# Two products on one moving operand: high and low activations side by side in the expert and FFN gate/up products

## The chip, the cores and the metric

One core of a Trainium2 chip runs the whole program in one launch. The metric is the device time of that launch in microseconds (us). The engines that matter are TensorE (PE, whose weight loads are listed as PEld), VectorE (DVE), ScalarE (ACT), GpSimd (POOL) and the DMA queue issued from SyncE (SP).

## The reference, cut to what matters

A sequence of 256 tokens with 1024 features passes through two blocks (latent attention with a PEER layer, gated linear attention with a PEER layer) and then a third block (two windowed attentions and a gated FFN). Everything is float32. The parts that the change touches:

```
def peer_ffn(x, w_query, sub_keys, u_tab, v_tab):     # twice; 128*128 experts, 8 heads, top 16
    ...                                               # query products, top-k, gates
    u = u_tab[idx]
    h = gelu(einsum('bthkd,btd->bthk', u, xi))
    w = gate * h
    return einsum('bthk,bthkd->btd', w, v_tab[idx])

u = silu(einsum('btd,df->btf', h, w_gate)) * einsum('btd,df->btf', h, w_up)   # FFN, 2816 hidden
x = x + einsum('btf,fd->btd', u, w_down)
```

## The kernel before, in words

**Weights as a stream of slabs.** All weights come through one stream of slabs of 128 x 1024 numbers (512 KB). SP loads slab n into one of 4 raw buffers. ACT makes its high part `hi` (`split_hi`, L248) in one of 3 buffers, once the slab three back is used up (semaphore `eaten`). DVE, or POOL for the PEER U slabs, makes the low part `lo` = raw - hi (`split_lo`, L257). Both parts are of the reduced-width float type fp32r. The activations are split in the same way into `xh` and `xl`, each of 8 chunks of 128 features x 256 tokens, by `Norm.high` (L349) and `Norm.low` (L356).

**PEER layer.** Instead of gathering experts it computes all of them: 8 query slabs, 128 U slabs and 128 V slabs per layer. `first(i)` on PE forms the 128 x 256 product of U slab i: for each of 8 chunks one matmul of `hi` with `xh` (L1245) and one of `hi` with `xl` (L1246), each with 256 moving columns; then, after a wait for `lo`, 8 matmuls of `lo` with `xh` (L1249). All 24 add up in the left half of PSUM bank i % 3, and the last one counts `eaten` up. During slabs 0 to about 40 DVE ranks the scores (`rank`).

**Gates, from slab 44 (LEAD).** Gates are built in 64 groups of 4 tokens. `GROUP_AT` gives a group to four of five slabs from 44 to 122, so a "group slab" has these steps: PE does 8 fp16 matmuls for the group (`sums`, L1272) after `first(i)`; DVE makes the one-hot tiles of the group two ahead (`one_hots`, L1502, L1504, L1506), multiplies the finished part of slab i by its gates (`gate_slab`, L1514) and applies the group's gates to all earlier slabs (`apply`, L1522). ACT does `split_hi` of the slab three ahead, then `bend(i)`: the Gelu of the product, of which the first `cut` tokens go back into PSUM in place (L1365) and the rest to `hidden` in SBUF (L1367). Then come `keep_sums` (L1373) and `low_gates` (L1384). `first(i)` may overwrite its bank when `gate_slab(i-3)` is done. `sums(g)` needs `one_hots(g)` and `low_gates(g)`, made two groups before.

**V slabs.** `second(v)` has 12 matmuls of 512 moving columns (L1285, L1286, L1292), with `pe_mh` and `pe_ml`, the split of `hidden[:, v]`, as weights.

**FFN.** The order of slabs is gate t, up t, down t-1, for 22 t. Gate and up are 24 matmuls of 256 columns each (`first` L2712, L2713 and `rest` L2720) into the two halves of bank t % 2; down is 12 of 512 columns (L2734 to L2736). ACT makes Silu of gate (L2770), DVE the product (L2787), ACT and DVE its split (L2774, L2790). All `split_lo` of the FFN are on DVE.

Other 512-column products are those of gated linear attention (`along`, L1702, L1704, L1710).

Of the kernel before, what the change touches and what calls it, by code (L numbers as in the profile page):

```python
# [17 lines left out]
P = 128  # L18
# [85 lines left out]
class Kernel:  # L104
    def __init__(self, nc, ctx, dram):
# [10 lines left out]
        self.xh = self.sb(ctx, "xh", [P, KD, T], F32R)  # L116
        self.xl = self.sb(ctx, "xl", [P, KD, T], F32R)
# [152 lines left out]
class Norm:  # L270
# [11 lines left out]
    def given_squares(self, act):  # L282
        k = self.k
        act.activation(k.xh[:, 0:4].rearrange("p c t -> p (c t)"), k.h[:, 0], ACT.Square, scale=D ** -0.5,
                       accum_out=k.mean[:, 0:1]).then_inc(self.squared.sem, 1)
# [8 lines left out]
    def given_diagonals(self, dve):  # L294
        k = self.k
        dve.tensor_tensor_reduce(
            out=k.xl[:, 0:4].rearrange("p c t -> p (c t)"), in0=k.h[:, 1], in1=k.h[:, 1], scale=1.0 / D, scalar=0.0,
            op0=ALU.mult, op1=ALU.add, accum_out=k.mean[:, 1:2]).then_inc(self.summed.sem, 1)
# [827 lines left out]
def peer(k, l, s0, norm, after):  # L1126
# [6 lines left out]
             "ranked", "turned", "equal", "hotted", "lowered", "summed", "spread", "applied", "bent", "gated", "m_hi", "m_lo")  # L1133
    (q_act, q_dve, zeroed, keyed, scored, s_act, s_dve, counted, raised, powered, ranked, turned, equal, hotted,
     lowered, summed, spread, applied, bent, gated, m_hi, m_lo) = (k.sig(f"pe_{x}") for x in names)
    hi, lo = k.hi, k.lo
    u0, v0, end = s0 + U0, s0 + V0, s0 + SLABS
    with ExitStack() as ctx:
# [8 lines left out]
        count = k.sb(ctx, "pe_count", [P, NK], I32)  # L1147

# [41 lines left out]
        with k.nc.Block() as block:  # L1190
# [11 lines left out]
            def _(pe):  # L1202
# [29 lines left out]
                def first(i):  # L1232
# [11 lines left out]
                    for c in range(KD):  # L1244
                        pe.matmul(ps, hi[:, r, c * P:(c + 1) * P], k.xh[:, c], start=(c == 0), stop=False)  # L1245
                        pe.matmul(ps, hi[:, r, c * P:(c + 1) * P], k.xl[:, c], start=False, stop=False)  # L1246
                    pe.wait_ge(*k.lo_at[u0 + i])
                    for c in range(KD):
                        last = pe.matmul(ps, lo[:, r, c * P:(c + 1) * P], k.xh[:, c], start=False, stop=(c == KD - 1))  # L1249
# [96 lines left out]
            def _(act):  # L1346
# [12 lines left out]
                def bend(i):  # L1359

                    g = grouped(i)
                    act.wait_ge(k.eaten, u0 + i + 1)
                    ps, cut = first_ps(i), g * GROUP
                    if cut:
                        last = act.activation(ps[:, 0:cut], ps[:, 0:cut], ACT.Gelu)  # L1365
                    if cut < T:
                        last = act.activation(hidden[:, i, cut:], ps[:, cut:], ACT.Gelu)  # L1367
# [66 lines left out]
            def _(dve):  # L1434
# [73 lines left out]

                def gate_slab(i):
# [36 lines left out]
                for i in range(LEAD, NK):  # L1546
                    g = GROUP_AT.get(i)
# [26 lines left out]
    gated.advance(NK - LEAD - 1)  # L1574
    for x in (equal, hotted, lowered, summed, spread, applied):
        x.advance(GROUPS)
# [516 lines left out]
def second_block(k, s0, norm, after):  # L2093
# [13 lines left out]
    with ExitStack() as ctx:  # L2107
# [73 lines left out]
        with k.nc.Block() as block:  # L2181
# [239 lines left out]
            def _(act):  # L2421
# [42 lines left out]
                for g in range(B2_SLABS):  # L2464
# [41 lines left out]
                    if g in (BB + 1, BB + 3):  # L2506
                        for m in ((g - BB - 1), (g - BB)):
                            act.wait_ge(y_done.sem, y_done.at(m + 1))
                            act.activation(k.xh[:, 2 * m:2 * m + 2].rearrange("p c t -> p (c t)"), yb[:, m], ACT.Copy)\
# [5 lines left out]
            def _(dve):  # L2515
# [60 lines left out]
                for g in range(B2_SLABS):  # L2576
# [44 lines left out]
                    if g in (BB + 1, BB + 3):  # L2621
# [8 lines left out]
                        for m in (2 * c, 2 * c + 1):  # L2630
                            dve.wait_ge(y_hi.sem, y_hi.at(m + 1))
                            dve.tensor_tensor(k.xl[:, 2 * m:2 * m + 2].rearrange("p c t -> p (c t)"), yb[:, m],
                                              k.xh[:, 2 * m:2 * m + 2].bitcast(F32).rearrange("p c t -> p (c t)"),
                                              ALU.subtract).then_inc(y_lo.sem, 1)
# [35 lines left out]
def ffn(k, s0, norm, out):  # L2670
# [3 lines left out]
    names = ("bent", "middle", "m_hi", "m_lo", "stepped", "done", "stored")  # L2674
    bent_up, middle, m_hi, m_lo, stepped, done, stored = (k.sig(f"ff_{x}") for x in names)
    order = ffn_order()
    end = s0 + len(order)
    with ExitStack() as ctx:
        bent = k.sb(ctx, "ff_bent", [P, 2, T])
        mid = k.sb(ctx, "ff_mid", [P, 2, T])  # L2680
        mh = k.sb(ctx, "ff_mh", [P, 2, T], F32R)
# [8 lines left out]
        with k.nc.Block() as block:  # L2690
# [14 lines left out]
            def _(pe):  # L2705
                def first(g, t, x, c0, c1):
# [3 lines left out]
                    for c in range(c0, c1):  # L2710
                        cols = slice(c * P, (c + 1) * P)
                        pe.matmul(first_ps(t, x), k.hi[:, r, cols], k.xh[:, c], start=(c == 0), stop=False)  # L2712
                        pe.matmul(first_ps(t, x), k.hi[:, r, cols], k.xl[:, c], start=False, stop=False)  # L2713

                def rest(g, t, x):
# [3 lines left out]
                    for c in range(KD):  # L2719
                        last = pe.matmul(first_ps(t, x), k.lo[:, r, c * P:(c + 1) * P], k.xh[:, c], start=False,  # L2720
                                         stop=(c == KD - 1))
                    last.then_inc(k.eaten, 1)
# [21 lines left out]
                for g, (kind, t) in enumerate(order):  # L2744
# [9 lines left out]
                    else:  # L2754
                        if kind == "gate" and t >= 2:
                            pe.wait_ge(middle.sem, middle.at(t - 1))
# [4 lines left out]
            def _(act):  # L2761
                norm.high(act, 0, KD)
                split_hi(k, act, s0 + 2)
                for g, (kind, t) in enumerate(order):
                    split_hi(k, act, s0 + g + RING)
                    if kind == "up":
                        act.wait_ge(k.eaten, s0 + g + 1)
# [9 lines left out]
            def _(dve):  # L2777
# [3 lines left out]
                for g, (kind, t) in enumerate(order):  # L2781
                    split_lo(k, dve, s0 + g + RING)
                    if kind == "up":
                        dve.wait_ge(bent_up.sem, bent_up.at(t + 1))
# [100 lines left out]
```

## Time and profile before

| | |
|---|---|
| median of 3 runs | 2291.86 us (2291.79 to 2295.11) |
| the profiled execution: its own time, its span | 2291.86 us, 2290.1 us |
| PE busy | 98% of the span |
| DVE, ACT, POOL busy | 61%, 54%, 31% |
| mean granted TensorE clock | 0.992 of full speed |

The profile's "busy" of PE counts each matmul from start to modelled end, and consecutive matmuls overlap, so 98% says only that PE is hardly ever without one. What a matmul costs in a dense stretch is the distance from its start to the next one's start.

### The profile page before, as it was taken

What the parts mean: (1) busy time and instruction counts of PE and PEld (TensorE: products, weight loads), DVE (VectorE), ACT (ScalarE), POOL (GpSimd) and SP (SyncE); (2) the same over time, 40 slices, a digit from 0 to 9 for tenths busy, and PEclk for the clock granted to TensorE, in tenths of its full rate; (3) what the DMA queues carried; (4) which work ended last, traced back from release to release, by engine and by line L of the source; (5) the groups of instructions that cost most, each with busy time, mean ns of one, the idle gap of its engine ahead of it and who ended that gap; (6) DMA issues with size and microseconds to landing.
All of it is one profiled execution on the core that took longest, in us unless ns stands there. A gap on an engine that the chain in (4) does not pass through costs nothing. (4 is left out here: it accounts for less than half of the span.)

```text
span 2290.1 us, 38835 instructions
## 1 busy us (share of the span) xinstructions
PE 2243.1 (98%) x15059; PEld 2025.1 (88%) x15059; DVE 1399.9 (61%) x2682; ACT 1236.2 (54%) x2448; POOL 704.2 (31%) x346
## 2 busy tenths in 40 slices
PE   8799999999999999999999999999999999999999
PEld 7679999999888888887999999988888888888998
DVE  6546965666555555565597566655555558446555
ACT  4434467777544444464446777754444454555443
POOL 3305877777200000001488777730000004000000
PEclk9889999999999999999999999999999999999999
DMA  5125655555566666563565555556666656424654
GB/s 166 56 66 162 183 177 161 162 162 159 180 185 186 190 186 187 153 179 109 156 183 178 160 164 159 165 175 185 187 189 185 188 162 225 124 85 162 187 185 148
DMA packets 122535, 375.55 MB, mean 164 GB/s; under 512 B 13024, under 2 KB 17376, under 8 KB 122352
## 3 DMA queue, kind: packets, MB, share of 16 engines
q1 hardware_dynamic: 122352, 373.06, 53.3%
q8 instruction: 121, 1.98, 0.3%
q14 instruction: 62, 0.51, 0.1%
HBM read 371.96 MB, written 1.05 MB: 163 GB/s over the span
## 5 line engine op out<-in xcount | busy, mean ns | idle before, releaser
L248 ACT ACTIVATE hi<-raw 128x1024 fp32r<-128x1024 f32 (+1 forms) x703 | 737.4, 1050 | 421.7 <-PE bank L1249 184.3
L257 DVE TENSOR_TENSOR lo<-raw,hi 128x1024 fp32r<-128x1024 f32 (+2 forms) x443 | 536.8, 1215 | 358.4 <-ACT hi L248 358.0
L257 POOL TENSOR_TENSOR lo<-raw,hi 128x1024 fp32r<-128x1024 f32 x260 | 630.7, 2429 | 252.8 <-ACT hi L248 252.8
L1245 PE MATMUL bank<-xh,hi 128*128 128x256 f32 x2048 | 512.3, 288 | 0.0
L1246 PE MATMUL bank<-xl,hi 128*128 128x256 f32 x2048 | 500.8, 283 | 0.0
L1285 PE MATMUL bank<-hi,pe_mh 128*128 128x512 f32 x1016 | 403.1, 397 | 1.1 <-DVE pe_ml L1528 1.1
L1286 PE MATMUL bank<-hi,pe_ml 128*128 128x512 f32 x1016 | 402.8, 396 | 0.0
L1246 PEld LDWEIGHTS bank<-xl,hi 128*128 128x128 f32 x2048 | 391.7, 191 | 0.1
L1245 PEld LDWEIGHTS bank<-xh,hi 128*128 128x128 f32 x2048 | 390.8, 191 | 0.1
L1396 ACT ACTIVATE pe_mh<-pe_hidden 128x256 fp32r<-128x256 f32 x256 | 107.0, 418 | 364.7 <-PE bank L1292 364.7
L320 POOL TENSOR_TENSOR rstd<-mean,minus_half 128x1 f32<-128x1 f32 x10 | 5.6, 556 | 964.4 <-DVE mean L327 964.2
L1249 PE MATMUL bank<-xh,lo 128*128 128x256 f32 x2048 | 287.0, 283 | 0.0
L1292 PE MATMUL bank<-lo,pe_mh 128*128 128x512 f32 x1016 | 279.2, 396 | 0.0
L1249 PEld LDWEIGHTS bank<-xh,lo 128*128 128x128 f32 x2048 | 264.2, 192 | 0.0
L1285 PEld LDWEIGHTS bank<-hi,pe_mh 128*128 128x128 f32 x1016 | 191.3, 188 | 48.4 <-DVE pe_ml L1528 1.9
L1292 PEld LDWEIGHTS bank<-lo,pe_mh 128*128 128x128 f32 x1016 | 191.4, 188 | 46.7
L1286 PEld LDWEIGHTS bank<-hi,pe_ml 128*128 128x128 f32 x1016 | 191.4, 188 | 46.5
L1528 DVE TENSOR_TENSOR pe_ml<-pe_hidden,pe_mh 128x256 fp32r<-128x256 f32 x256 | 108.8, 425 | 160.7 <-ACT pe_mh L1396 160.7
L1384 ACT ACTIVATE pe_hot_l<-bank,pe_slots 128x128 f16<-128x128 f32 x512 | 146.2, 369 | 89.7 <-DVE pe_hot_h L1506 89.7
L1502 DVE TENSOR_TENSOR bank<-bank,pe_slots 128x512 f32<-128x512 f32 x128 | 89.5, 699 | 139.6 <-PE bank L1272 139.5
L1514 DVE TENSOR_TENSOR pe_hidden<-pe_hidden,bank 128x256 f32<-128x256 f32 (+47 forms) x166 | 47.8, 288 | 84.7 <-ACT pe_hidden L1367 65.7
L2712 PE MATMUL bank<-xh,hi 128*128 128x256 f32 x352 | 86.5, 283 | 0.9 <-ACT xh L349 0.9
(396 smaller groups left out, 3223.9 us busy)
## 6 DMA issues: line engine op xcount, KB each, us to landing
raw<-in_peer_u SPq DMA_DIRECT2D x256, 512.0 KB, 3.6
raw<-in_peer_v SPq DMA_DIRECT2D x256, 512.0 KB, 4.3
raw<-in_w_gate_up SPq DMA_DIRECT2D x44, 512.0 KB, 3.7
raw<-in_w_in SPq DMA_DIRECT2D x34, 512.0 KB, 4.1
raw<-in_gla_w_in SPq DMA_DIRECT2D x24, 512.0 KB, 4.3
raw<-in_w_down SPq DMA_DIRECT2D x22, 512.0 KB, 3.6
raw<-in_w_query SPq DMA_DIRECT2D x16, 512.0 KB, 3.4
raw<-in_mla_w_o SPq DMA_DIRECT2D x8, 512.0 KB, 3.5
```

The lines of the kernel that those rows point to most:

```text
L248: act.activation(k.hi[:, n % RING, 0:x * e], k.raw[:, n % RAW, 0:x * e], ACT.Copy).then_inc(k.hi_done, 1)
L257: eng.tensor_tensor(k.lo[:, n % RING, 0:x * e], k.raw[:, n % RAW, 0:x * e], k.hi[:, n % RING, 0:x * e].bitcast(F32), ALU.subtract).then_in ...
L1245: pe.matmul(ps, hi[:, r, c * P:(c + 1) * P], k.xh[:, c], start=(c == 0), stop=False)
L1246: pe.matmul(ps, hi[:, r, c * P:(c + 1) * P], k.xl[:, c], start=False, stop=False)
L1249: last = pe.matmul(ps, lo[:, r, c * P:(c + 1) * P], k.xh[:, c], start=False, stop=(c == KD - 1))
L1285: pe.matmul(second_ps(a, c), mh[:, v % 2, tok], hi[:, r, half], start=(v == 0), stop=False)
L1286: pe.matmul(second_ps(a, c), ml[:, v % 2, tok], hi[:, r, half], start=False, stop=False)
L1292: last = pe.matmul(second_ps(a, c), mh[:, v % 2, tok], lo[:, r, half], start=False, stop=(v == NK - 1))
L1384: last = act.activation(hot_l[:, g % 2, t], hot_ps(g)[:, t * NK:(t + 1) * NK], ACT.Copy, scale=slots[:, 3, c:c + 1])
L1396: act.activation(mh[:, v % 2], hidden[:, v], ACT.Copy).then_inc(m_hi.sem, 1)
L1502: dve.tensor_tensor(hot_ps(g)[:].rearrange("p (t i) -> p t i", t=GROUP), each, over(0, g), ALU.is_equal).then_inc(equal.sem, 1)
L1528: dve.tensor_tensor(ml[:, v % 2], hidden[:, v], mh[:, v % 2].bitcast(F32), ALU.subtract)\
```

## The change

- `xh` and `xl` become two views of one tile `xx` of 8 chunks x 2 x 256: chunk c of `xh` and chunk c of `xl` lie side by side.
- For U slabs 44 to 127 (84 of 128 in each of the two PEER layers), and for the FFN's gate and up slabs (44), the two matmuls per chunk on `hi` become one matmul with 512 moving columns. It writes a whole PSUM bank: the left half gets hi x xh, the right half hi x xl. The 8 matmuls of `lo` with `xh` stay at 256 columns into the left half. The last chunk's 512-column matmul comes after them. A slab has 16 matmuls in place of 24, and as many columns.
- DVE adds the two halves (`fold`, a `tensor_reduce` over 512 numbers per partition) into a new SBUF tile `whole`, before its other work of the slab. The Gelu and Silu wait for it and read `whole`; the Gelu of the first `cut` tokens still goes to PSUM, where `gate_slab` reads it.
- In the FFN gate and up have a bank each (banks 0 to 3), DVE's fold comes ahead of `split_lo` of the slab, and the product reads `whole`.

```
-        self.xh = self.sb(ctx, "xh", [P, KD, T], F32R)
-        self.xl = self.sb(ctx, "xl", [P, KD, T], F32R)
+        self.xx = self.sb(ctx, "xx", [P, KD, 2, T], F32R)
+        self.xh, self.xl = self.xx[:, :, 0], self.xx[:, :, 1]
...
+        whole = k.sb(ctx, "pe_whole", [P, 2, T])
...
+                    if i >= LEAD:
+                        for c in range(KD - 1):
+                            pe.matmul(k.bank[i % 3][:], hi[:, r, c * P:(c + 1) * P],
+                                      k.xx[:, c].rearrange("p s t -> p (s t)"), start=(c == 0), stop=False,
+                                      skip_group_check=True)
...
+                    if i >= LEAD:
+                        last = pe.matmul(k.bank[i % 3][:], hi[:, r, (KD - 1) * P:KD * P],
+                                         k.xx[:, KD - 1].rearrange("p s t -> p (s t)"), start=False, stop=True,
+                                         skip_group_check=True)
                     last.then_inc(k.eaten, 1)
...
                 def bend(i):
...
+                    if i >= LEAD:
+                        act.wait_ge(folded.sem, folded.at(i - LEAD + 1))
+                    else:
+                        act.wait_ge(k.eaten, u0 + i + 1)
+                    made = whole[:, i % 2] if i >= LEAD else ps
                     if cut:
-                        last = act.activation(ps[:, 0:cut], ps[:, 0:cut], ACT.Gelu)
+                        last = act.activation(ps[:, 0:cut], made[:, 0:cut], ACT.Gelu)
...
+                def fold(i):
+
+                    dve.wait_ge(k.eaten, u0 + i + 1)
+                    if i >= LEAD + 2:
+                        dve.wait_ge(bent.sem, bent.at(i - 1))
+                    dve.tensor_reduce(whole[:, i % 2], k.bank[i % 3][:].rearrange("p (s t) -> p t s", s=2), AX_X, ALU.add)\
+                       .then_inc(folded.sem, 1)
...
                 for i in range(LEAD, NK):
+                    fold(i)
...
         def first_ps(t, x):
-            return k.bank[t % 2][:, x * T:(x + 1) * T]
+            return k.bank[t % 2 * 2 + x][:, 0:T]
...
-                        act.activation(bent[:, t % 2], first_ps(t, 0), ACT.Silu).then_inc(bent_up.sem, 1)
+                        act.activation(bent[:, t % 2], whole[:, t % 2, 0], ACT.Silu).then_inc(bent_up.sem, 1)
...
                 for g, (kind, t) in enumerate(order):
+                    if kind != "down":
+                        dve.wait_ge(k.eaten, s0 + g + 1)
+                        if t >= 2:
+                            dve.wait_ge(bent_up.sem, bent_up.at(t - 1))
+                            dve.wait_ge(middle.sem, middle.at(t - 1))
+                        dve.tensor_reduce(whole[:, t % 2, int(kind == "up")],
+                                          both_ps(t, int(kind == "up")).rearrange("p (s t) -> p t s", s=2), AX_X,
+                                          ALU.add).then_inc(folded.sem, 1)
                     split_lo(k, dve, s0 + g + RING)
...
-                        dve.tensor_tensor(mid[:, t % 2], bent[:, t % 2], first_ps(t, 1), ALU.mult)\
+                        dve.tensor_tensor(mid[:, t % 2], bent[:, t % 2], whole[:, t % 2, 1], ALU.mult)\
                            .then_inc(middle.sem, 1)
```

## Rows read from the trace of the kernel before

**Rows 1.** The page: busy time of PE, and granted clock by slices.
```profile
PE 2243.1 (98%) x15059; PEld 2025.1 (88%) x15059; DVE 1399.9 (61%) x2682; ACT 1236.2 (54%) x2448; POOL 704.2 (31%) x346
...
PEclk9889999999999999999999999999999999999999
```

**Rows 2.** Busy PE, PEld, DVE, ACT, POOL, clock, DMA: U slabs from 44, FFN.
```profile
319.50:590.00 270.50, 270.50 (x2502) 267.75 (x2501) 164.30 (x335) 195.97 (x565) 198.54 (x83) 1.00 0.54 162
...
2100.00:2284.00 184.00, 183.91 (x1297) 172.59 (x1298) 96.31 (x109) 81.54 (x109) 0.00 (x0) 1.00 0.56 175
```

**Rows 3.** Timeline of PE: starts of slabs 44, 126 and 127, first layer.
```profile
324.22 0.28 PE L1245 MATMUL bank<-xh,hi 128*128 128x256 f32 x1
...
592.38 0.28 PE L1245 MATMUL bank<-xh,hi 128*128 128x256 f32 x1
...
594.30 1.12 PE L1249 MATMUL bank<-xh,lo 128*128 128x256 f32 x8
...
595.26 0.28 PE L1245 MATMUL bank<-xh,hi 128*128 128x256 f32 x1
```

**Rows 4.** Timeline of PE: 512-column matmuls of linear attention, and of V.
```profile
993.97 0.40 PE L1702 MATMUL bank<-hi,xh 128*128 128x512 f32 x1
...
995.81 1.07 PE L1710 MATMUL bank<-lo,xh 128*128 128x512 f32 x4
...
1001.25 1.07 PE L1710 MATMUL bank<-lo,xh 128*128 128x512 f32 x4
...
700.22 0.39 PE L1285 MATMUL bank<-hi,pe_mh 128*128 128x512 f32 x1
...
702.09 1.10 PE L1292 MATMUL bank<-lo,pe_mh 128*128 128x512 f32 x4
```

**Rows 5.** Timeline of PE in the FFN: a down slab and the next gate slab.
```profile
2110.24 0.39 PE L2734 MATMUL bank<-hi,ff_mh 128*128 128x512 f32 x1
...
2113.04 0.28 PE L2712 MATMUL bank<-xh,hi 128*128 128x256 f32 x1
...
2114.95 1.12 PE L2720 MATMUL bank<-xh,lo 128*128 128x256 f32 x8
```

**Rows 6.** Timeline of DVE: its work in group slab 120, start and duration in us.
```profile
577.21 0.70 DVE L1502 TENSOR_TENSOR bank<-bank,pe_slots 128x512 f32<-128x512 f32 x1 [0.62 <-PE bank L1272]
577.82 0.68 DVE L1504 TENSOR_TENSOR pe_hot_j<-bank,pe_slots 128x512 f16<-128x512 f32 x1
578.42 0.68 DVE L1506 TENSOR_TENSOR pe_hot_h<-bank,pe_slots 128x512 f16<-128x512 f32 x1
579.02 0.40 DVE L1514 TENSOR_TENSOR pe_hidden<-pe_hidden,bank 128x244 f32<-128x244 f32 x1
579.33 0.65 DVE L1522 SCALAR_TENSOR_TENSOR pe_hidden<-bank,pe_hidden 128x484 f32<-128x484 f32 x1
```

**Rows 7.** DVE: `apply` and a reduction (ns min/median/max), a PSUM copy of 512.
```profile
L1522 DVE SCALAR_TENSOR_TENSOR pe_hidden<-bank,pe_hidden x128: 333/500/664, 329.6 to 1506.7; 128x180 f32<-128x180 f32 x2, 128x184 f32<-128x184 f32 x2, 128x188 f32<-128x188 f32 x2, 128x192 f32<-128x192 f32 x2
...
L888 DVE TENSOR_REDUCE ml_sums<-ml_sq x8: 674/813/954, 39.8 to 88.0; 128x8 f32<-128x512 f32 x4, 128x8 f32<-128x768 f32 x4
...
L1448 DVE COPY pe_hidden<-bank 128x512 f32<-128x512 f32 x8 | 5.5, 692 | 19.8 <-PE bank L1228 19.8
```

**Rows 8.** Timeline of ACT in slab 120; low parts made by POOL (ns).
```profile
579.13 1.14 ACT L1384 ACTIVATE pe_hot_l<-bank,pe_slots 128x128 f16<-128x128 f32 x4 [0.85 <-DVE pe_hot_h L1506]
580.15 1.08 ACT L248 ACTIVATE hi<-raw 128x1024 fp32r<-128x1024 f32 x1
...
L257 POOL TENSOR_TENSOR lo<-raw,hi x260: 2380/2400/6075, 30.8 to 1512.3; 128x1024 fp32r<-128x1024 f32 x130
```

**Rows 9.** Timeline at the seam from U to V, and at the FFN's t = 20.
```profile
598.83 0.50 PE L1285 MATMUL bank<-hi,pe_mh 128*128 128x512 f32 x1 [0.53 <-DVE pe_ml L1528]
...
2272.63 0.39 PE L2734 MATMUL bank<-hi,ff_mh 128*128 128x512 f32 x1
...
2276.02 0.42 DVE L2790 TENSOR_TENSOR ff_ml<-ff_mid,ff_mh 128x256 fp32r<-128x256 f32 x1 [0.48 <-ACT ff_mh L2774]
```

More of the change, by code:

```diff
@@ L1361, in bend @@
                     g = grouped(i)
-                    act.wait_ge(k.eaten, u0 + i + 1)
+                    if i >= LEAD:
+                        act.wait_ge(folded.sem, folded.at(i - LEAD + 1))
+                    else:
+                        act.wait_ge(k.eaten, u0 + i + 1)
                     ps, cut = first_ps(i), g * GROUP
+                    made = whole[:, i % 2] if i >= LEAD else ps
                     if cut:
-                        last = act.activation(ps[:, 0:cut], ps[:, 0:cut], ACT.Gelu)
+                        last = act.activation(ps[:, 0:cut], made[:, 0:cut], ACT.Gelu)
                     if cut < T:
-                        last = act.activation(hidden[:, i, cut:], ps[:, cut:], ACT.Gelu)
+                        last = act.activation(hidden[:, i, cut:], made[:, cut:], ACT.Gelu)
                     last.then_inc(bent.sem, 1)
@@ L2670, in ffn @@
 def ffn(k, s0, norm, out):
-    names = ("bent", "middle", "m_hi", "m_lo", "stepped", "done", "stored")
-    bent_up, middle, m_hi, m_lo, stepped, done, stored = (k.sig(f"ff_{x}") for x in names)
+    names = ("bent", "folded", "middle", "m_hi", "m_lo", "stepped", "done", "stored")
+    bent_up, folded, middle, m_hi, m_lo, stepped, done, stored = (k.sig(f"ff_{x}") for x in names)
     order = ffn_order()
@@ L2680, in ffn @@
         mid = k.sb(ctx, "ff_mid", [P, 2, T])
+        whole = k.sb(ctx, "ff_whole", [P, 2, 2, T])
         mh = k.sb(ctx, "ff_mh", [P, 2, T], F32R)
@@ L2709, in first @@
                     pe.wait_ge(k.hi_done, s0 + g + 1)
-                    for c in range(c0, c1):
+                    for c in range(c0, min(c1, KD - 1)):
                         cols = slice(c * P, (c + 1) * P)
-                        pe.matmul(first_ps(t, x), k.hi[:, r, cols], k.xh[:, c], start=(c == 0), stop=False)
-                        pe.matmul(first_ps(t, x), k.hi[:, r, cols], k.xl[:, c], start=False, stop=False)
+                        pe.matmul(both_ps(t, x), k.hi[:, r, cols], k.xx[:, c].rearrange("p s t -> p (s t)"),
+                                  start=(c == 0), stop=False, skip_group_check=True)
                 def rest(g, t, x):
@@ L2719, in rest @@
                     for c in range(KD):
-                        last = pe.matmul(first_ps(t, x), k.lo[:, r, c * P:(c + 1) * P], k.xh[:, c], start=False,
-                                         stop=(c == KD - 1))
-                    last.then_inc(k.eaten, 1)
+                        pe.matmul(first_ps(t, x), k.lo[:, r, c * P:(c + 1) * P], k.xh[:, c], start=False, stop=False,
+                                  skip_group_check=True)
+                    pe.matmul(both_ps(t, x), k.hi[:, r, (KD - 1) * P:KD * P],
+                              k.xx[:, KD - 1].rearrange("p s t -> p (s t)"), start=False, stop=True,
+                              skip_group_check=True).then_inc(k.eaten, 1)
                 def second(g, t):
@@ L2754, in _ @@
                     else:
-                        if kind == "gate" and t >= 2:
-                            pe.wait_ge(middle.sem, middle.at(t - 1))
+                        if t >= 2:
+                            pe.wait_ge(folded.sem, folded.at(2 * (t - 2) + int(kind == "up") + 1))
                         first(g, t, kind == "up", 0, KD)
```

31 lines of the change are left out of this document (18 added, 13 removed).

## The prediction, made before the result

> **What bounds the kernel now.** I read the page first: PE is busy for 98% of the span and the others for at most 61%, and the granted clock is at its full level, the 2.4 GHz one, in all but the first slices [rows 1]. Then the busy time by stage, for the two stages that the change touches: PE is busy without a gap, at clock 1.00, while DVE has 164 of 270 us, ACT 196 and POOL 199 [rows 2]. A stage whose PE is never without a matmul can still be one in which PE waits a little each time, so I read the timeline for the distance between starts. From the start of slab 126 to that of 127 it is 595.26 - 592.38 = 2.88 us, and the eight matmuls of `lo` take (1.12 - 0.28) / 7 = 0.120 us each [rows 3]. 24 x 0.120 = 2.88: a plain U slab is 24 matmuls end to end with nothing between them. From slab 44 to the first V matmul less its own wait there are 598.83 - 0.53 - 324.22 = 274.1 us [rows 3, 9]; 84 slabs of 2.88 make 241.9, and the other 32.2 us are 64 groups at 0.50 us, the fp16 matmuls of `sums`. So PE sets the pace in all of this stage. The FFN shows the same: a down slab of (2113.04 - 2110.24) / 12 = 0.233 us a matmul, then a gate slab at 0.119 to 0.120 [rows 5]. What the change is worth is therefore what it takes from PE's distances, less any new wait.
>
> **The matmuls.** The change leaves the number of columns alone (24 x 256 = 16 matmuls with 8 x 512 + 8 x 256) and takes away 8 starts a slab. At the 2.4 GHz level 256 columns are 106.7 ns and 512 are 213.3. The measured distances exceed them: 120 - 106.7 = 13.3 ns at 256 columns [rows 3]. At 512 columns there are three readings. In linear attention, in a long dense run, it is (1.07 - 0.39) / 3 = 0.227 us, an excess of 13.4. The first eight of such a run, right behind 256-column matmuls, take (995.81 - 993.97) / 8 = 0.230. In the V stage it is (702.09 - 700.22) / 8 = 0.234, for the whole stage [rows 4]. The FFN's down slabs, which stand between 256-column slabs, are at 0.233, and the 16 matmuls behind them at (2114.95 - 2113.04) / 16 = 0.119 [rows 5].
> The new slab is 7 matmuls of 512, 8 of 256, 1 of 512. No row has this mixture. Its bounds: 8 x 0.227 + 8 x 0.119 = 2.768 us, or 8 x 0.234 + 8 x 0.120 = 2.832. I take 0.231 for a 512, near the 0.230 of a run just behind 256-column ones, because every run of the new slab is that short, with a step toward the FFN's 0.233; and 0.1194 for a 256. That is 1.848 + 0.955 = 2.803 us, **0.077 us less than 2.88** (bounds 0.048 and 0.112).
>
> A rule speaks against this. The Trainium skill, TensorE: Matmul & The Clock Gate, section Back-to-back issue gap, gives the distance of matmuls in a warm array as columns / 2.4 + 2.5 ns, so that a merged pair would save only 2.5 ns: 20 ns a slab, and 4.2 us in all instead of 16.1. The rows have an excess of 13.3 at 256 columns, so the measurement decides here against the rule; it is weighed again among the rivals.
>
> **How many slabs gain.** 84 in each of two layers and 44 in the FFN: 212. Three of them don't gain. In each layer PE already waits 0.53 us at the first V matmul for DVE's `pe_ml` [rows 9]; that chain starts at `eaten` of slab 126 (the Gelu of 126, `gate_slab`, `split_lo`, `split_middle`), so a shorter slab 127 only makes the wait 0.08 longer. The first gate slab of the FFN is given out piece by piece as the norm's chunks come. 209 x 0.077 = **16.1 us** (bounds 209 x 0.048 = 10.0 and 209 x 0.112 = 23.4).
>
> **The fold on DVE: hidden.** It reads 512 numbers of PSUM and writes 256. A copy of 512 out of PSUM takes 0.69 us, a reduction of 512 numbers at least 0.674 [rows 7]; consecutive DVE instructions start 0.08 us before the end of the one before (577.21, 577.82, 578.42 [rows 6]), so it adds about 0.60. `apply` reads PSUM with a step of 128 numbers and has 484 columns in 0.65 [rows 6], so a step alone isn't dear. In slab 120, the last one with all of DVE's work, the three one-hot tiles, `gate_slab` and `apply` take 577.21 to 579.98, 2.77 us, behind an idle 0.62 us that `sums` ends [rows 6]. The fold is released earlier, by `eaten`, ahead of `sums`: it falls into that idle time nearly exactly. DVE's chain becomes 0.60 + 2.77 = 3.37 us, against a PE period of 2.80 + 0.50 = 3.30. So late in the stage DVE falls back 0.07 us a slab, for four slabs, and gains it back in the fifth, which has only a fold and `gate_slab`, 1.0 us. Early in the stage `apply` takes 0.33 instead of 0.65 [rows 7] and `gate_slab` next to nothing, and the chain is 2.8. Being late by 0.3 us costs nothing: `gate_slab(120)` is done at 579.42, and PE needs it for slab 123, which starts near 583.7 (`sums` of slab 120 ends some 0.3 us ahead of 577.21, where slab 121 begins, and two periods of 3.38 follow); the last one-hot tile is done at 579.10, `low_gates` on ACT at 580.27 [rows 6, 8], and PE needs both two groups on, near 583.2. With that cover gone, every 0.1 us would cost PE 0.1 us.
>
> **What is queued behind the new waits.** ACT's `bend` waits for the fold (about 0.7 us behind `eaten`) in place of `eaten`. Ahead of it ACT does `split_hi`, 1.08 us from the same `eaten` [rows 8], so the fold is there first. Behind it stand `keep_sums` and `low_gates`; the latter already waits 0.85 us for DVE's one-hot tile [rows 8], which comes up to 0.1 us later, and the next `split_hi` with it. Its high part isn't needed for two more slabs. POOL's low part, 2.40 us a slab [rows 8], keeps below the new 2.80. The Gelu reads SBUF in place of PSUM; ACT has 196 of 270 us [rows 2], and 0.05 us more on each stays inside its idle time. The loads wait for the low parts as before; the DMA share is 0.54 [rows 2], 0.56 after.
>
> **FFN.** DVE has 96 of 184 us there [rows 2], 4.5 us of a period of 8.55; two folds make 5.7. For t = 20 the product's low part ends at 2276.02 + 0.42, 3.8 us behind the end of the up slab (2272.63) [rows 9], and is needed 8.5 us behind it. With a fold of 0.6 ahead of it, still hidden. For the last t only one down slab, 2.80 us, lies between, but its chain has no `split_lo` or `split_hi` in it any more: Silu, product and split are under 2 us, with the fold 2.5. It costs nothing; if that is wrong, some 0.3 us once.
>
> **The sum.** The profiled execution took 2291.86 us, which is also the median. 2291.9 - 16.1 = **2275.8 us**, with bounds 2281.9 and 2268.5.
>
> **The rivals.**
> *A: group slabs keep their period.* DVE's chain of 3.37 us, or ACT's behind it, sets 128 group slabs at the present 3.38 us and only the plain slabs and the FFN gain: 128 x 0.077 = 9.9 us are lost, 2285.7. For it: the chain is longer than the new period late in the stage. Against: 2.9 to 4.2 us of slack and a light fifth slab.
> *B: the excess goes with the columns.* If 13.3 ns per 256 columns are lost for what is streamed and not for a start, a 512 takes 240 and nothing is gained: 2291.9. The V stage's 0.234 leans that way, the 0.227 of linear attention stands against it. The skill's rule comes out beside it by another way, at 2287.7.
> *C, slower: the fold at half speed.* It would take 1.38 us, 1.30 from start to start, if reading two numbers 1 KB apart in PSUM breaks DVE's pace. Five slabs then cost DVE 4 x 2.77 + 0.42 + 6.5 = 18.0 us at the end of the stage and 15.4 at its start (2.2 in place of 2.77, 0.1 in place of 0.42), against PE's 16.0. It exceeds PE over the last 77% of the stage, by 1.0 on their mean, so 0.77 over all 16 such fives of each layer: 32 x 0.77 = 24.6 us, 2300.4. It decides from a fold of about 1.2 us on. Against it: `apply`'s step of 512 bytes at full pace.
>
> **Chances and range.** My forecast 0.77, A 0.10, B with the rule beside it 0.08, C 0.05. What a measurement of this kernel can tell from no change is about 0.2%, 4.6 us. Forecast and A are faster, B is the same, C is slower; a few in a hundred of each go over the edge: faster 0.87, same 0.07, slower 0.06. Range 2267 to 2287: the bounds with a little over at the fast end, and A; B, C and the rule lie outside. The forecast alone: 2268.5 to 2281.9.
>
> **What the profile after would show.** Starts of plain slabs 2.77 to 2.83 us apart and of group slabs 0.50 more; 512-column rows 0.227 to 0.234 apart. Folds of 0.65 to 0.70 us, with no idle PE behind `pe_hidden` or `pe_hot_l`. DVE busy up by 212 x 0.68 = 144 us. The FFN's period 8.55 - 0.15 = 8.40. PE's wait at the first V matmul about 0.6. Wrong would be: a fold above 1 us, PE waits inside U, a 512 at 0.238 or more, or 256-column matmuls that get slower behind the wide ones.

## The result, and the profile after

| | before | after |
|---|---|---|
| median | 2291.82 us (2290.35 to 2295.11, 4 runs) | 2275.45 us (2274.55 to 2279.9, 4 runs) |
| ratio | | 0.9931, 95% interval 0.9915 to 0.9947 |
| span of the profiled execution | 2290.1 us | 2273.0 us |

The change made the kernel 16.4 us faster by the medians and 17.1 by the spans; 2275.8 was forecast, from a gain of 16.1.

The page after, the line that answers to [rows 1]: 1696 matmuls fewer (212 slabs of 8).
```profile
PE 2225.8 (98%) x13363; PEld 1928.5 (85%) x13363; DVE 1534.6 (68%) x2894; ACT 1243.0 (55%) x2448; POOL 704.8 (31%) x346
```
By stage (busy PE, PEld, DVE, ACT, POOL, clock, DMA), beside [rows 2]: PE is still without a gap in the U slabs, with 1892 matmuls in 271 us where it had 2502 in 270.5. The load share there is 0.51; the prediction had 0.56. DVE went up from 164 to 218 us there, and from 96 of 184 to 127 of 181 in the FFN.
```profile
319.00:590.00 271.00, 271.00 (x1892) 236.17 (x1891) 217.91 (x422) 203.04 (x571) 201.23 (x84) 1.00 0.51 166
2085.00:2266.00 181.00, 180.34 (x953) 154.34 (x952) 127.29 (x156) 83.69 (x111) 0.00 (x0) 1.00 0.54 178
```
Timeline of PE, slab 44's start and then slabs 126 and 127 with the seam to V, beside [rows 3, 9]:
```profile
324.11 1.78 PE L1247 MATMUL bank<-xx,hi 128*128 128x512 f32 x7
...
585.60 1.77 PE L1247 MATMUL bank<-xx,hi 128*128 128x512 f32 x7
...
588.39 1.77 PE L1247 MATMUL bank<-xx,hi 128*128 128x512 f32 x7
590.00 1.11 PE L1256 MATMUL bank<-xx,lo 128*128 128x256 f32 x8
590.95 0.39 PE L1259 MATMUL bank<-xx,hi 128*128 128x512 f32 x1
591.97 0.50 PE L1297 MATMUL bank<-hi,pe_mh 128*128 128x512 f32 x1 [0.62 <-DVE pe_ml L1552]
```
A plain slab takes 588.39 - 585.60 = 2.79 us, where it was 2.88. From slab 44 to the first V matmul there are 591.97 - 324.11 = 267.86 us; before it was 598.83 - 324.22 = 274.61, so this stage gave 6.75 us. The second layer gave the same (6.77 from the first low part to the last, in both layers). The wait at the first V matmul is 0.62, where it was 0.53.

Timeline of PE in the FFN, beside [rows 5]: an up slab, a down slab's first and last matmul, the next gate slab and up slab. One period of three slabs is 2101.99 - 2093.61 = 8.38 us, where it was 8.55, and from the first low part to the last the stage took 175.97 us, where it was 179.57: 3.6 less. Together 2 x 6.75 + 3.6 = 17.1 us, the whole difference of the spans.
```profile
2093.61 1.77 PE L2741 MATMUL bank<-xx,hi 128*128 128x512 f32 x7
...
2096.40 0.39 PE L2765 MATMUL bank<-hi,ff_mh 128*128 128x512 f32 x1
...
2098.98 0.40 PE L2767 MATMUL bank<-hi,ff_ml 128*128 128x512 f32 x1
2099.21 1.75 PE L2741 MATMUL bank<-xx,hi 128*128 128x512 f32 x7
...
2101.99 1.77 PE L2741 MATMUL bank<-xx,hi 128*128 128x512 f32 x7
```
The folds, by tile (busy us, mean ns of one, idle ahead of it): 0.69 us each, 146.7 us in all, while DVE's total went up by only 134.7 (from 1399.9 to 1534.6). The other work of DVE did not shrink: the durations of all its instructions, added up one by one, rose by 149.0. The total counts time once in which two instructions overlap, and a fold of 0.69 overlaps the next instruction by about 0.09 us.
```profile
L1530 DVE TENSOR_REDUCE pe_whole<-bank 128x256 f32<-128x512 f32 x168 | 116.3, 692 | 65.1 <-PE bank L1259 62.6
...
L2818 DVE TENSOR_REDUCE ff_whole<-bank 128x256 f32<-128x512 f32 x44 | 30.4, 691 | 12.9 <-PE bank L2751 12.9
```
Timeline of DVE late in the stage, beside [rows 6]: `apply`, a fold directly behind it, which was released while DVE was still at work, and then an idle 1.05 us. DVE is late by a little and has it back in a slab without one-hot tiles; PE has no wait there.
```profile
573.02 0.66 DVE L1546 SCALAR_TENSOR_TENSOR pe_hidden<-bank,pe_hidden 128x484 f32<-128x484 f32 x1
573.61 0.69 DVE L1530 TENSOR_REDUCE pe_whole<-bank 128x256 f32<-128x512 f32 x1
575.35 0.41 DVE L1538 TENSOR_TENSOR pe_hidden<-pe_hidden,bank 128x248 f32<-128x248 f32 x1 [1.05 <-ACT pe_hidden L1383]
```

### The profile page after: what moved, and what is told of

Read it like the earlier page. It is cut to its first block and busy times, and to the rows that moved or that the text cites. A ratio compares the mean times of both kernels' runs of the same rounds, so it can differ in the third digit from the quotient of the medians.

```text
span 2273.0 us, 35881 instructions
## 1 busy us (share of the span) xinstructions
PE 2225.8 (98%) x13363; PEld 1928.5 (85%) x13363; DVE 1534.6 (68%) x2894; ACT 1243.0 (55%) x2448; POOL 704.8 (31%) x346
## 3 DMA queue, kind: packets, MB, share of 16 engines
HBM read 371.96 MB, written 1.05 MB: 164 GB/s over the span
## 5 line engine op out<-in xcount | busy, mean ns | idle before, releaser
L1247 PE MATMUL bank<-xx,hi 128*128 128x512 f32 x1176 | 307.2, 400 | 0.0
L1256 PE MATMUL bank<-xx,lo 128*128 128x256 f32 x2048 | 286.2, 283 | 0.0
L1256 PEld LDWEIGHTS bank<-xx,lo 128*128 128x128 f32 x2048 | 274.2, 191 | 13.1
L1247 PEld LDWEIGHTS bank<-xx,hi 128*128 128x128 f32 x1176 | 211.5, 189 | 36.8
L1252 PE MATMUL bank<-xx,hi 128*128 128x256 f32 x704 | 173.6, 284 | 0.0
L1253 PE MATMUL bank<-xx,hi 128*128 128x256 f32 x704 | 172.7, 283 | 0.0
L1530 DVE TENSOR_REDUCE pe_whole<-bank 128x256 f32<-128x512 f32 x168 | 116.3, 692 | 65.1 <-PE bank L1259 62.6
L1253 PEld LDWEIGHTS bank<-xx,hi 128*128 128x128 f32 x704 | 135.1, 192 | 0.1
L1252 PEld LDWEIGHTS bank<-xx,hi 128*128 128x128 f32 x704 | 135.1, 192 | 0.1
```

The lines of the kernel that those rows point to most:

```text
L1247: pe.matmul(k.bank[i % 3][:], hi[:, r, c * P:(c + 1) * P], k.xx[:, c].rearrange("p s t -> p (s t)"), start=(c == 0), stop=False, skip_grou ...
L1530: dve.tensor_reduce(whole[:, i % 2], k.bank[i % 3][:].rearrange("p (s t) -> p t s", s=2), AX_X, ALU.add)\
```

## The experiments

What had to be told apart: whether the gain is the number of starts (forecast) or something else that came with the edit; whether the fold is hidden with much room or little; and why a 512-column matmul takes 227 ns in one stage and 234 in another, which had been three readings without a reason. Each kernel is the kernel after with one thing edited, but for two that measure PE by itself.

### Two narrow matmuls in place of one wide

Every 512-column matmul on `hi` is split into two of 256 into the two halves of the bank. Fold, waits, tiles and banks stay.

```
-  pe.matmul(k.bank[i % 3][:], hi[...], k.xx[:, c].rearrange("p s t -> p (s t)"), ...)
+  pe.matmul(k.bank[i % 3][:, 0:T], hi[...], k.xh[:, c], ...)
+  pe.matmul(k.bank[i % 3][:, T:2 * T], hi[...], k.xl[:, c], ...)
```

> The changed kernel, but each 512-column matmul is split again into two of 256 columns: hi times xh into the left half of the bank, hi times xl into the right half. The fold, the waits and the banks stay. Forecast's theory (each start of a matmul costs about 13 ns over its columns, the fold is hidden): plain U slabs go back to 2.88 us, group slabs to 3.38, the FFN period to 8.55, and the time to 2291 to 2293 us, that of the kernel before. Rival (the gain comes from where the products are added up, or from the fold that takes PSUM reads off the ScalarE path, not from the number of starts): slabs stay at 2.80 and the time near 2275.5. If the fold had a hidden price that the wide matmuls pay for, the time would be above 2294.

Measured: 2292.04 us (2290.07 to 2295.93, 10 runs), ratio to before 1.0004 (0.9995 to 1.0014). Slabs are 2.88 us apart again, group slabs 3.38, the FFN's period 8.55. DVE does the same folds as in the kernel after. Line of its folds, and its U stage:
```profile
L1532 DVE TENSOR_REDUCE pe_whole<-bank 128x256 f32<-128x512 f32 x168 | 116.2, 692 | 80.4 <-PE bank L1262 77.8
```
```profile
319.00:590.00 271.00, 271.00 (x2506) 268.25 (x2505) 214.69 (x417) 199.43 (x565) 198.67 (x83) 1.00 0.53 162
```
So the whole gain is in the number of matmuls that PE starts, and everything else of the change costs nothing that can be measured, with PE never idle in this stage either way. Each matmul of these kernels loads its weights anew (as many weight loads as matmuls, [rows 1] and the page after), so the change took away 8 loads a slab together with 8 starts. Which of the two the 13.3 ns belong to isn't separated by any run.

### The fold done twice

One more fold per U slab into a tile that nobody reads.

```
+  dve.tensor_reduce(spoilt[:, i % 2], halves, AX_X, ALU.add)
   dve.tensor_reduce(whole[:, i % 2], halves, AX_X, ALU.add).then_inc(folded.sem, 1)
```

> The changed kernel with a second, useless fold ahead of each fold in the two PEER layers (same read of PSUM, written to a tile nobody reads); the FFN as it was. Rival C of the prediction as an experiment: a fold of 1.2 us from start to start. Its sum (VectorE needs 17.5 us per five slabs at the end of the stage, 14.9 at its start, against 16.0 of TensorE) says that VectorE sets the pace over the last 58% of the stage and 13.9 us are lost: 2289. If a fold's time goes straight into the path of each group slab, 128 x 0.6 = 77 us: 2352. If there is more slack than the sum says, 2275 to 2278.

Measured: 2295.47 us (2292.89 to 2296.71, 10 runs), ratio to before 1.0008 (0.9998 to 1.0017): 20.0 us above the kernel after, by medians and spans alike. From the first low part to the last there are 272.15 us per layer, 7.9 more, and to the first V matmul 8.6 more. All slabs keep 3.30 and 2.79 up to about slab 86, half way; from then on the last two of each four group slabs are 3.5 to 4.05 apart. The expected loss was 13.9 us and a time of 2289: the slabs lost 2 x 7.9 = 15.7, near it, but the sum had left out two things. At each seam to V, PE waits for DVE's `pe_ml` ahead of the first two V slabs (0.62 us and next to nothing in the kernel after) and comes out 1.44 us later, 2.9 in all. The other 1.4 or so are the clock's: late in the last block this profile has two stretches of 3.4 us at a granted clock of 0.50 (the second is below), where the profile of the kernel after has one.
```profile
600.54 0.50 PE L1298 MATMUL bank<-hi,pe_mh 128*128 128x512 f32 x1 [1.46 <-DVE pe_ml L1554]
...
604.08 0.50 PE L1298 MATMUL bank<-hi,pe_mh 128*128 128x512 f32 x1 [0.47 <-DVE pe_ml L1554]
...
2018.30:2021.70 3.40, 3.40 (x18) 3.40 (x18) 0.51 (x4) 1.10 (x4) 0.00 (x0) 0.50 0.20 78
```
The timeline of DVE late in the U stage shows what bounds it there: seven instructions end to end, 570.18 - 566.33 = 3.85 us for a slab, each fold 0.60 from start to start.
```profile
566.33 0.68 DVE L1532 TENSOR_REDUCE pe_spoilt<-bank 128x256 f32<-128x512 f32 x1
566.93 0.68 DVE L1533 TENSOR_REDUCE pe_whole<-bank 128x256 f32<-128x512 f32 x1
567.53 0.69 DVE L1519 TENSOR_TENSOR bank<-bank,pe_slots 128x512 f32<-128x512 f32 x1
568.13 0.68 DVE L1521 TENSOR_TENSOR pe_hot_j<-bank,pe_slots 128x512 f16<-128x512 f32 x1
568.72 0.68 DVE L1523 TENSOR_TENSOR pe_hot_h<-bank,pe_slots 128x512 f16<-128x512 f32 x1
569.32 0.39 DVE L1540 TENSOR_TENSOR pe_hidden<-pe_hidden,bank 128x232 f32<-128x232 f32 x1
569.62 0.64 DVE L1548 SCALAR_TENSOR_TENSOR pe_hidden<-bank,pe_hidden 128x468 f32<-128x468 f32 x1
570.18 0.68 DVE L1532 TENSOR_REDUCE pe_spoilt<-bank 128x256 f32<-128x512 f32 x1
```
and PE's timeline beside it, at `sums`:
```profile
566.84 0.22 PE L1285 MATMUL bank<-pe_hot_h,pe_hot_j 128*128 128x128 f16 x1 [0.37 <-ACT pe_hot_l L1401]
```
So 0.60 us more on DVE is too much, and the one fold of the change is free. Rival C (a fold of 1.38 us, 2300.4) was a mechanism of this kernel; what spared it is the fold's own 0.69.

### The fold behind the one-hot tiles

The same work, only `fold(i)` moved from ahead of `one_hots` to behind it in DVE's order.

```
-                    fold(i)
                     g = GROUP_AT.get(i)
                     if g is not None and g + 2 < GROUPS:
                         one_hots(g + 2)
+                    fold(i)
```

> The changed kernel with the fold behind the one-hot tiles in VectorE's order, in place of ahead of them. Theory 1 (what counts is the total of VectorE's work and two slabs of slack on TensorE): no change, 2275 to 2277. Theory 2 (the order makes a ring: one-hot tiles 1.8 us, fold 0.6, then Gelu and the sums' copy on ScalarE 0.8 to 0.9, then gate_slab and apply 0.4 to 1.0 on VectorE, and only then the next one-hot tiles): 3.6 to 4.1 us a group slab against 3.30; with the lighter fifth slab some 25 us are lost, 2300, and the trace has VectorE idle ahead of gate_slab.

Measured: 2308.58 us (2306.94 to 2311.25, 4 runs), ratio to before 1.0068 (1.0051 to 1.0085). It costs 33 us against the kernel after, more than the second fold, though DVE does no more work. Group slabs are late from about slab 57 on (3.67 to 3.95 us for two of four, and near the end of the stage for a third), 16.5 us per layer. The waits (us in total, times, the longest in us) show a ring: ACT's Gelu waits for the fold, and DVE's `gate_slab` for that Gelu.
```profile
ACT bank L1381 <- DVE pe_whole L1530: 155.0, 126, 1.9
DVE pe_hidden L1538 <- ACT pe_hidden L1383: 108.5, 156, 1.4
```
In the kernel after the same view has ACT wait for DVE's one-hot tile, as before:
```profile
ACT pe_hot_l L1400 <- DVE pe_hot_h L1522: 79.7, 124, 1.1
```
The theory of the ring was right in kind and a quarter too small in size (about 25 us expected, 33 measured). Of the cover that the prediction leaned on, the fold's place ahead of `sums` is therefore as much a part as its length.

### Where do 227 and 234 ns come from? PE by itself

Two kernels that leave out the whole computation: stretches of 96 matmuls each, all weights from one tile, all moving columns from another. One run of each.

> None of the reference's work: stretches of 96 matmuls with nothing to wait for, first with the other engines idle, then once more with ScalarE and VectorE copying and subtracting 128x1024 tiles beside them. 256 columns into one bank; 512 columns into one, two or four banks; 512 columns with four weight tiles used over and over; the order of the V stage; eight of 512 and eight of 256 in turn; 512 columns that add up. Theory 1 (four PSUM banks in turn make the V stage's 234 ns): 120 ns for 256 columns, 227 for one and two banks, 234 for four and for the V order. Theory 2 (weight tiles that come back at once): 234 for four weight tiles and the V order, 227 else. Theory 3 (the other engines' SBUF traffic): 227 everywhere in the first round, 234 in the second. The mixed stretch is 174 ns on the mean by the forecast's numbers, and 180 if the excess went with the columns.

Measured: every stretch of 512-column matmuls at 226.7 to 227 ns, with one, two or four banks, eight or four weights, or in V's order, and the same with ACT and DVE at work; 256-column ones at 120.0. The mixture of the new slab (eight wide, eight narrow) had its own pattern: behind the switch to wide 233, 236, 228, 233, 230, then 227; behind the switch to narrow 113, 119, then 120. Its mean is 174.3 ns, (146.62 - 129.89) / 96, against the expected 174 and the 180 of rival B; 16 of them make the 2.79 us of a slab.
```profile
129.89 4.32 PE L2896 MATMUL bank<-b_mv,b_wh 128*128 128x512 f32 x22
...
146.62 1.55 PE L2901 MATMUL bank<-b_mv,b_wh 128*128 128x512 f32 x6
```

Timeline of PE, one stretch of 512-column matmuls and the next: (201.83 - 194.81) / 31 = 0.2265.
```profile
194.81 7.19 PE L2872 MATMUL bank<-b_mv,b_wh 128*128 128x512 f32 x31
201.83 13.54 PE L2876 MATMUL bank<-b_mv,b_wh 128*128 128x512 f32 x59
```

> None of the reference's work: again stretches of 96 matmuls of 512 columns, now adding up in PSUM as in the V stage, over one, two, three and four banks, in the V stage's order, in that order with a semaphore count on every twelfth, two banks for 12 matmuls and then the other two, and the V order without adding. First with the other engines idle, then beside ScalarE, VectorE and loads of 512 KB slabs at full pace. Theory 1 (adding up over four banks makes the V stage's 234 ns): 227 up to two banks, 234 for four banks and the V order, 227 without adding; two by two tells whether 12 at a time are enough. Theory 3 (the loads and the other engines): 227 throughout the first round, 234 in the second. Theory 4 (it is the semaphores): only the stretch with counts differs.

Measured: 226.7 ns in all stretches again, with sums kept open in one to four banks, with counts, two by two, each started afresh, in silence and beside loads of 178 GB/s, ACT and DVE. None of the theories named so far holds: order, banks, accumulation, counts and the traffic of other engines don't give 234 in these benches.

### V's stage changed inside the kernel

First other weights: `xh` and `xl` in place of `pe_mh` and `pe_ml` (so V computes another product).

```
-  pe.matmul(second_ps(a, c), mh[:, v % 2, tok], hi[:, r, half], ...)
+  pe.matmul(second_ps(a, c), k.xh[:, v % KD, tok], hi[:, r, half], ...)
```

> The changed kernel, but 127 of the 128 V slabs of each layer take chunks of xh and xl as weights in place of pe_mh and pe_ml, which ScalarE and VectorE rewrite in every slab; all waits, banks and moving operands stay, and the output is not the reference's. The stretches by themselves did not show the V stage's 234 ns. Theory 5 (weight tiles that are rewritten beside the matmuls cost the 7.6 ns): V matmuls go to 227, slabs from 2.81 to 2.72 us, the time by 254 x 0.09 = 23 us to 2252. Rival (banks, waits or moving operand): 2.81 and 2275.

Measured: 2251.53 us in one run, 24 us below the kernel after; V's distance 226.7. The FFN's down slabs, not edited, stay at 233 to 236. So it is something about these two tiles.

Then V's four sums put into two banks, which adds the two halves of the features into one sum, the weights as they were:

> The changed kernel, but 127 of the 128 V slabs of each layer add both halves of the features into the same two banks in place of four; the output is not the reference's. Theory 1 in place (four banks cost the 7.6 ns, but only beside the real waits): slabs of 2.72 us and 2252. Rival: 2.81 and 2275.

Measured: 2273.18 us in one run, V's distance 234.3. Banks are out for the second time.

Then the tiles kept and their numbers changed: `mh` is filled from `xh` in place of `hidden` (V computes another product).

> The changed kernel, but ScalarE fills mh of the V slabs from a chunk of xh in place of the gated hidden values, in the same tile at the same time; ml is the difference to hidden as before; the output is not the reference's. Theory 7 (the values in the weights set the distance): V slabs of 2.72 us and 2251. Theories 5 and 6: 2.81 and 2275.

Measured: 2277.84 us in one run, V's distance 234.3. The numbers are out. (That the time is 2 us above the kernel after says nothing: this run's mean clock was 0.989, and the kernel after took 2276.25 at 0.990 and 2274.66 at 0.992.)

Then the numbers kept and the tiles moved: `mh` and `ml` are allocated once, right behind `xx` and ahead of `raw`, and shared by the PEER layers and the FFN.

```
         self.xx = self.sb(ctx, "xx", [P, KD, 2, T], F32R)
+        self.mh = self.sb(ctx, "mh", [P, 2, T], F32R)
+        self.ml = self.sb(ctx, "ml", [P, 2, T], F32R)
...
-        mh = k.sb(ctx, "pe_mh", [P, 2, T], F32R)
-        ml = k.sb(ctx, "pe_ml", [P, 2, T], F32R)
+        mh, ml = k.mh, k.ml
```

> The changed kernel with one edit: the weight tiles of the V and FFN down slabs (mh, ml) lie ahead of the raw, hi and lo buffers in SBUF, right behind xx, in place of behind the 128 KB of hidden; nothing else moves in order or size. Theory 5 (it is that they are rewritten beside the matmuls): V slabs stay at 2.81 us and the time at 2275. Theory 6 (it is where they lie in SBUF): V slabs of 2.72 us, a down slab's matmuls near 229, and 23 to 25 us less, 2251.

Measured: **2251.2 us** (2250.15 to 2253.76, 4 runs), ratio to before 0.9825 (0.9809 to 0.9842). V's distance is 226.7, FFN down's median 227. It beats both kernels, by where two tiles lie.

### Where exactly? Unused tiles as shims

A tile of 32 bytes a partition, and for the control one of 64, ahead of the small scalar tiles, so that everything behind moves by that much.

```
+        self.pad = self.sb(ctx, "pad", [P, 8])        # 16 in the second kernel
         self.minus_half = self.sb(ctx, "minus_half", [P, 64])
```

> The kernel after, with an unused tile of 32 bytes in each partition laid ahead of the small scalar tiles, so that the two tiles of V's weights (high and low of the masked numbers) lie 32 bytes further on in SBUF, nothing else moved on the engines. Theory 8 (what costs V's matmuls 7.6 ns each is how the weight tile's start stands to a multiple of 64 bytes; in the kernel after it stands 32 bytes off from how hi, lo and xx stand): the distance in V's stages is 226.7 ns, FFN down's 227, the time 2251 us (2249 to 2254), as with the weights allocated ahead of raw. Rival (the region of SBUF in which the tiles lie, or what else lies near them, decides): V's distance stays at 234.3 ns and the time is 2275 us (2273 to 2278).

> The control: the same unused tile with 64 bytes, so that the weight tiles are moved twice as far and stand to a multiple of 64 bytes as in the kernel after. Theory 8: V's distance 234.3 ns, the time 2275 us. Rival (any shift of the tiles changes it, or the region decides): by the first half of it 226.7 ns and 2251 us, by the second 234.3 ns in both runs.

Measured: with 32 bytes 2273.51 us (2272.63 to 2273.86, 4 runs), V's distance 232.4; with 64 bytes 2277.57 in one run (clock 0.989 again), 233.3. Theory 8 falls: with 32 bytes the tiles stood to 64 bytes as all others, and V was still not at 226.7. The rival in its plain form falls as well, since the shims did change the distances, if little. The U stage moved too, its mean from 229.1 to 231.3 ns in both, although neither of its operands had been moved.

The addresses in the partition that the allocator gave were the next thing to look at. Their differences can be worked out from the sizes of the tiles in order:

| where | weights start at, modulo 256 | moving operand, modulo 256 | difference | distance |
|---|---|---|---|---|
| after, U and FFN gate | `hi` 45824: 0 | `xx` 13056: 0 | 0 | 226.7 behind the first five |
| after, V | `pe_mh` 213600: 96 | `hi`: 0 | 96 | 234.3 |
| after, FFN down | `ff_mh` 79968: 96 | `hi`: 0 | 96 | 233.5 to 235.4 |
| weights from `xh` | 13056: 0 | `hi`: 0 | 0 | 226.7 |
| `mh` ahead of `raw` | 29440: 0 | `hi` 49920: 0 | 0 | 226.7 |
| the benches | 79968: 96 | 84064: 96 | 0 | 226.7 |
| 32 bytes | 213632: 128 | `hi`: 0 | 128 | 232.4 |
| 64 bytes | 213664: 160 | `hi`: 0 | 160 | 233.3 |

It can't be the region, for the benches had their weights where `ff_mh` lies. What all the rows at 226.7 share is the difference. The table leaves out two readings, and they don't fit a rule of the difference alone: U with either shim (difference 0, 231.3 ns between the wide matmuls of a slab) and, with 64 bytes, the FFN's gate slab behind a down slab (difference 0; 230, 235, 234, 236, 224, 231, 235 ns). The last kernel was made to test whether moving the weight tiles to a difference of 0 is enough, with the tiles left at the far end:

```
+        k.sb(ctx, "pe_pad", [P, (40, 104)[l]])
         mh = k.sb(ctx, "pe_mh", [P, 2, T], F32R)
...
+        k.sb(ctx, "ff_pad", [P, 40])
         mh = k.sb(ctx, "ff_mh", [P, 2, T], F32R)
```

> The kernel after, with unused tiles laid directly ahead of the weight tiles pe_mh and ff_mh, so that these stay at the far end of SBUF and move by 160 bytes in the first PEER layer and in FFN and by 416 bytes in the second layer. Counted from the addresses of the allocator, the distance from the moving operand (hi) to the weights, modulo 256 bytes, was 0 wherever a run showed 226.7 ns (U, FFN gate, V with weights in xh, V with mh ahead of raw, and the bench, whose two tiles both lay 96 off a multiple of 256), and 96, 128 and 160 where it showed 234.3 (after), 232.4 (e10_pad_32) and 233.3 (e11_pad_64). Theory 9 (that difference decides): V's distance is 226.7 ns in the first layer (difference 0, and 0 modulo 512 too), FFN down's 227; in the second layer 226.7 if the period is 256 bytes and over 231 if it is 512 (difference 256). The time is 2251 us (2249 to 2254) with a period of 256 and about 2262 with one of 512. Rival (the region in which the tiles lie, near or far from xx and hi): 231 to 235 ns in all three places and 2273 to 2278 us.

Measured: 2251.62 us (2249.91 to 2253.9, 4 runs), ratio to before 0.9826 (0.981 to 0.9842). Timeline of PE in V's first layer. In the kernel after, from the second matmul of a slab to the first of the next there are 11 distances, (701.84 - 699.26) / 11 = 0.2345:
```profile
699.26 0.39 PE L1298 MATMUL bank<-hi,pe_ml 128*128 128x512 f32 x1
...
701.84 0.40 PE L1297 MATMUL bank<-hi,pe_mh 128*128 128x512 f32 x1
```
In this kernel, a whole slab, (702.61 - 699.89) / 12 = 0.2267:
```profile
699.89 0.39 PE L1298 MATMUL bank<-hi,pe_mh 128*128 128x512 f32 x1
...
701.70 1.07 PE L1305 MATMUL bank<-lo,pe_mh 128*128 128x512 f32 x4
702.61 0.39 PE L1298 MATMUL bank<-hi,pe_mh 128*128 128x512 f32 x1
```
The second layer, where the difference is 0 modulo 256 and 256 modulo 512, gives (1601.74 - 1600.38) / 6 = 0.2267 as well:
```profile
1600.38 0.39 PE L1298 MATMUL bank<-hi,pe_mh 128*128 128x512 f32 x1
...
1601.74 0.39 PE L1298 MATMUL bank<-hi,pe_mh 128*128 128x512 f32 x1
```
Theory 9's forecast came true in all three places, with a period of 256 bytes (128 is excluded by the row of 32 bytes), and the rival of the region fell. 3048 V matmuls at 7.6 ns are 23.2 us and 264 of the FFN at 5.9 (234.2 to 228.3 in the mean) another 1.5; the spans differ by 24.4.

One rival is left nearly untouched. In every kernel that computes, the moving operand of these matmuls started at a multiple of 256 bytes, so where the difference was 0 the weights' own start was such a multiple too. Only the benches (both operands at 96) speak for the difference and against the weights' own start, and no bench was run with the weights at 96 and the moving operand at 0, to show that it can be slow at all.

## Why the prediction was right, step by step

- **What bounds.** PE's distances set the pace, with no idle time to take away. Right: splitting the wide matmuls lost all of the gain again with the same DVE work.
- **The matmuls.** Forecast 2.803 us a slab and 0.077 saved, measured 2.79 and in the mean of 83 distances 6.77 / 83 = 0.082. Between the wide matmuls of a U slab there are 229.1 ns in the mean (231 forecast) and behind the last one 233.3; a narrow one takes 119.1 (119.4 forecast). That difference is the whole difference between 16.1 and 17.1 us: 209 x 0.082 = 17.1.
- **The reason for 231 was partly wrong.** I leaned on the FFN's down slabs at 0.233, as matmuls that stand between narrow ones. Nearly all of their excess has to do with where their weight tiles lie, and little with neighbours: with the tiles moved their median is 227 and their mean 228.3. Being behind narrow ones costs only a run-in of some five matmuls. The eight wide ones of a plain slab take (2.79 - 0.953) / 8 = 0.230 each, the reading of linear attention's first eight, which was the right row to go by; the step from 0.230 to 0.231 came from the wrong one. The same goes for V's 0.234 [rows 4], which I had read as a sign for rival B.
- **How many gain.** 209 of 212; the seam's wait became 0.62 ("about 0.6").
- **The fold.** Forecast 0.60 from start to start and 0.65 to 0.70 long, measured 0.60 and 0.69. Hidden, as forecast, and by a margin smaller than one more fold. "From a fold of about 1.2 us on" (rival C) was too generous: by the prediction's own sum DVE passes PE's 16.0 us for five slabs at the end of the stage once a fold adds (16.0 - 11.5) / 5 = 0.9 us, and 1.2 us cost 20. Group slabs came out at 3.30, which was the period that I had weighed DVE's 3.37 against.
- **FFN.** Forecast 8.40, measured 8.38. Durations of the folds: 144 forecast, 147 measured; DVE's busy time rose by 135, since neighbours overlap.
- **The rivals.** A: group slabs went from 3.38 to 3.30, so it fell. B: the excess stays 13.3 ns a matmul, at 256 columns (120.0 - 106.7) and at 512 (226.67 - 213.33), both in the bench. C: the fold at full pace; the doubled fold shows that it would have bitten. The rule of the Trainium skill, TensorE: Matmul & The Clock Gate, section Back-to-back issue gap, would have 2.5 ns in place of the 13.3; the bench and the gain decide against it for these operands. The section gives this rule for an isolated matmul and says that in a stream with weight loads both operations set the spacing, as in all the streams here.

## What to carry to other kernels

Where PE has no idle time, look at the distance between starts and subtract the columns: with fp32r operands here 13.3 ns a matmul were left. Halving the count of matmuls at equal columns gets most of it back: 8 x 13.3 ns are 0.107 us a slab, and 0.082 were gained in the mean. In a plain slab the rest is what the switches of width cost: some 27 ns over the first five wide matmuls, less the 8 that the switch back returns. It pays as long as the work that the merge puts on another engine falls into that engine's idle time at the moment when it is released. The order on that engine mattered more than its length here: the same fold three instructions later cost twice the gain. When like matmuls take different times in different stages, compare the starts of weights and moving operand, modulo 256 bytes, before looking for contention: pads of 160 and 416 bytes were worth 24 us, more than the whole change.

## What the runs showed of the hardware that I had not expected

- A 512-column fp32r matmul in a dense run of its like takes 226.7 ns when the start of its weight tile and that of its moving operand differ by a multiple of 256 bytes in the partition, and 232.4 to 234.3 when they differ by 96, 128 or 160. Whether it is the difference or the weights' own start rests on the benches alone. What in the chip does this isn't shown. Other differences weren't tried, nor 256-column matmuls.
- In the slow case the distances aren't even but repeat: 234, 235, 233, 232, 238, 237, 231 ns over and over through the first V stage of the kernel after (234, 235, 234, 231, 238, 237, 231 in the second), and 232, 237, 231 with the shim of 64 bytes; in the good case they are 226 and 227 throughout. A pattern of seven doesn't follow the 12 matmuls of a slab.
- Behind a switch from narrow to wide matmuls the first five take 233, 235, 229, 232 and 231 ns and the rest 227. With the shims of 32 and 64 bytes this run-in lasted through the slab behind a group (230, 231, 236, 228, 233, 231), although U's own operands lay as before; the tiles of the fp16 matmuls ahead of it had moved. Whether these matter isn't tried.
- DVE adds two numbers of PSUM 1 KB apart at the pace of a copy (0.69 us for 512 numbers).
- The excess of 13.3 ns is there at the full clock, and at the half clock it is gone, in the one stretch looked at. Where the granted clock is 0.50 (the 1.2 GHz level; the kernel after, from 1991.2 to 1994.6 us), 256-column matmuls with a weight load each are (1993.57 - 1991.86) / 8 = 0.214 us apart, and 256 / 1.2 is 213.3 ns.
```profile
1991.20:1994.60 3.40, 3.40 (x18) 3.40 (x17) 0.00 (x0) 0.00 (x0) 0.00 (x0) 0.50 0.00 0
...
1991.86 0.41 PE L2231 MATMUL bank<-xx,hi 128*128 128x256 f32 x1
...
1993.57 0.41 PE L2231 MATMUL bank<-xx,hi 128*128 128x256 f32 x1
```
